# Output projection: two plain tiles and eight pairs by seven products, in place of four and seven

## The reference, cut to what matters

```python
    m = g_a * (y_a @ w_proj_a) + g_b * (y_b @ w_proj_b)
    return x + gate * (m @ w_out), k, v
...
y_prompt = rmsnorm(x, final_g)
y_sample = rmsnorm(z, final_g)
```

## Time and profile before

| | us |
|---|---|
| median of 3 runs | 1726.87 (1726.21 to 1728.54) |
| the profiled execution's own time | 1724.92 |
| its span | 1723.1 |
| TensorE busy in the span | 1690.2 (98%) |
| VectorE busy | 1245.8 (72%) |
| ScalarE busy | 861.1 (50%) |
| GpSimd busy | 655.3 (38%) |

### The profile page before, as it was taken

One profiled execution on the slowest core, in us unless ns is written; L12 is line 12 of the kernel. 1 busy time (PEld: TensorE's weight loads), 2 busy tenths in 40 slices (PEclk: granted clock), 3 DMA queues, 4 the chain that ended last, 5 costly groups with the idle time before them and its releaser, 6 DMA issues.

```text
span 1723.1 us, 27518 instructions
## 1 busy us (share of the span) xinstructions
PE 1690.2 (98%) x9835; PEld 1434.0 (83%) x9835; DVE 1245.8 (72%) x1785; ACT 861.1 (50%) x1497; POOL 655.3 (38%) x509
## 2 busy tenths in 40 slices
PE   5999999999999999999999999999999999999998
PEld 3787888888899988878888888888988888888886
DVE  3785788788656858888687855777777665678776
ACT  3553444455577644434544437777779222333443
POOL 0044675565200027865555653224223100005443
PEclk9999999999999999999999999999999999999999
DMA  9443534333598725434333369888766777673442
GB/s 326 125 148 128 134 125 142 95 92 110 177 320 258 208 92 134 158 124 110 99 125 102 104 167 222 229 224 192 169 145 174 246 235 229 189 263 129 152 159 86
DMA packets 271644, 286.31 MB, mean 166 GB/s; under 512 B 49960, under 2 KB 217748, under 8 KB 268309
## 3 DMA queue, kind: packets, MB, share of 16 engines
q1 hardware_dynamic: 270146, 276.31, 53.6%
q10 hardware_dynamic: 1363, 8.24, 2.1%
HBM read 203.18 MB, written 81.30 MB: 165 GB/s over the span
## 4 chain that ended last, share of the span: by engine, by line
PE 93%; DMA 2%; DVE 1%; issue 1%; ACT 1%; SPq 1%; POOL 1%; ACTq 0%; POOLq 0%; DVEq 0%
PE banks L1803 45%; PE banks L2361 6%; PE banks L2939 4%; PE banks L2941 4%; PE banks L2940 4%; PE banks L3000 3%; PE banks L3001 3%; PE banks L2999 3%; PE banks L2325 2%; PE banks L1933 2%; PE banks L1932 2%; PE banks L1931 2%; PE banks L2331 2%; PE banks L2301 1%; PE banks L2302 1%
## 5 line engine op out<-in xcount | busy, mean ns | idle before, releaser
L1803 PE MATMUL banks<-a_hi,w_hi 128*128 128x512 f32 x1176 | 460.2, 391 | 1.1 <-ACT out_stage L1121 0.4
L1803 PE MATMUL banks<-a_hi,w_lo 128*128 128x512 f32 x1176 | 457.9, 389 | 0.0
L1803 PE MATMUL banks<-a_lo,w_hi 128*128 128x512 f32 x1176 | 457.7, 389 | 0.0
L1494 DVE SCALAR_TENSOR_TENSOR banks<-glu_out,taps,banks 128x1009 f32<-128x1009 f32 (+1 forms) x240 | 342.2, 1426 | 5.3
L1803 PEld LDWEIGHTS banks<-a_hi,w_hi 128*128 128x128 f32 x1176 | 220.8, 188 | 50.2 <-issue 4.0
L1803 PEld LDWEIGHTS banks<-a_hi,w_lo 128*128 128x128 f32 x1176 | 220.7, 188 | 46.5
L1803 PEld LDWEIGHTS banks<-a_lo,w_hi 128*128 128x128 f32 x1176 | 220.8, 188 | 45.2
L1005 POOL TENSOR_TENSOR t_raw<-w_raw 128x512 f32<-128x512 f32 x39 | 53.7, 1377 | 396.5 <-DMA w_raw<-in_w_in 390.3
L1413 DVE SCALAR_TENSOR_TENSOR w_lo<-w_raw,w_hi 128x1024 fp32r<-128x1024 f32 x84 | 112.0, 1334 | 106.4 <-ACT w_hi L1095 105.1
L959 POOL TENSOR_TENSOR w_lo<-t_raw,w_hi 128x1024 fp32r<-128x1024 f32 x70 | 171.5, 2458 | 28.1 <-ACT w_hi L1095 25.8
L2473 ACT ACTIVATE probs<-scores,stat 128x640 f32<-128x640 f32 (+2 forms) x128 | 106.7, 833 | 50.6 <-DVE stat L2395 49.2
(11 more groups left out here) (276 smaller groups left out, 3660.2 us busy)
## 6 DMA issues: line engine op xcount, KB each, us to landing
w_raw<-in_w_in SPq DMA_DIRECT2D x34, 1024.0 KB, 5.6
cw_raw<-in_w_in SPq DMA_DIRECT2D x44, 512.0 KB, 5.1
proj<-out_stage SPq DMA_DIRECT2D x80, 256.0 KB, 2.2
gates_in<-proj SPq DMA_DIRECT2D x64, 256.0 KB, 3.1
q_split<-q_rows SPq DMA_DIRECT2D x8, 1152.0 KB, 6.0
w_ada<-in_w_ada SPq DMA_DIRECT2D x8, 1024.0 KB, 10.9
w_raw<-in_w_in SPq DMA_DIRECT2D x16, 512.0 KB, 4.8
q_rows<-out_stage_r SPq DMA_DIRECT2D x64, 128.0 KB, 2.4
```

Source lines behind the costliest of these rows:

```text
L1494: op = dve.scalar_tensor_tensor(dst, src, by, dst, ALU.mult, ALU.add)
L1803: op = pe.matmul(out, x[w][:, b, k], y, start=(start and k == j == 0), stop=(k == H - 1 and j == 2), skip_group_check=not start)
```

## The change

One pair more, two plain tiles less. Plain are now tiles 14 and 15; tiles 16 and 17 (the context) are the last pair. The first 256 columns of m's block 4 stay in SBUF (`mo_hi` and `mo_lo` are half as large), its last 256 are stored to memory by `store_m`, and `load_m_pair` for the first two pairs waits for the stores of all five blocks. The operands of the first pair lie elsewhere: A11, S1 and A12 need no plain tile to be done, S2 and S3 the first, S4 and A22 the second. The order of the preparing calls on ScalarE, VectorE and GpSimd is rewritten, and the loads of the weight blocks and of x are issued among the stores of block 4. Some waits of the first pair for units that are no more are left out.

```diff
 RING = [4, 5, 0, 1, 2, 3]
-OUT_BANKS = [6, 7, 4, 5, 0, 1, 2, 3]
-OUT_TILES = list(range(14, NTOK)) + list(range(14))
-PLAIN = 4
-OUT_UNITS = [(0, 0), (0, 1), (1, 0), (1, 1), (2, 0), (2, 1), (3, 1), (3, 0)]
+OUT_BANKS = [6, 7, 2, 3]
+OUT_TILES = [14, 15] + list(range(14)) + [16, 17]
+PLAIN = 2
+OUT_UNITS = [(0, 0), (0, 1), (1, 1), (1, 0)]
 NU, NE = len(OUT_UNITS), (NTOK - PLAIN) // 2
...
 Z_AT = {(part, e): NU + 4 * e + i + 1 for e in range(NE) for i, part in enumerate(PARTS)}
-SLOT_TILE = {"A11": 0, "S1": 0, "S2": 1, "A12": 1, "S3": 2, "S4": 2, "A22": 3}
+SLOT_TILE = {"S2": 0, "S3": 0, "S4": 1, "A22": 1}
 SUMS = {"S1": ("A21", "A22"), "S2": ("S1", "A11"), "S3": ("A11", "A21"), "S4": ("A12", "S2")}
 T_SUMS = {"T1": ("B12", "B11"), "T3": ("B22", "B12"), "T2": ("B22", "T1"), "T4": ("B21", "T2")}
-T_HIGHS, T_LOWS = ["T1", "T3", "T2", "T4"], ["T1", "T3", "T2", "T4"]
+T_HIGHS, T_LOWS = ["T1", "T3", "T2", "T4"], ["T1", "T2", "T3", "T4"]
 POOL_SUMS = [("T2", 0), ("T4", 0)] + [(s, e) for e in range(NE) for s in ("S1", "S2", "S3", "S4")]
...
         (wo_hi, wo_lo, wo_raw)[h % 3][h // 3] = at(f"wo{h // 3}_{kind}", [P, KC, 512], where, dtype)
-    mo_hi, mo_lo = at("mo_hi", [P, 4, KC, P], X_AT + 16384, F32R), at("mo_lo", [P, 4, KC, P], ln_at, F32R)
+    mo_hi, mo_lo = at("mo_hi", [P, PLAIN, KC, P], X_AT + 16384, F32R), at("mo_lo", [P, PLAIN, KC, P], ln_at, F32R)
     w_half = {"B11": (0, 0), "B21": (0, 1), "B12": (1, 0), "B22": (1, 1)}
...
     t_hi, t_lo, s_raw = {}, {}, {}
-    for n, where in (("A11", X_AT + 16384), ("S1", ln_at), ("S2", X_AT + 20480), ("A12", ln_at + 4096), ("S3", X_AT + 24576),
-                     ("S4", ln_at + 8192), ("A22", X_AT + 28672)):
+    for n, where in (("A11", X_AT + 24576), ("S1", X_AT + 28672), ("S2", X_AT + 16384), ("A12", ln_at + 8192), ("S3", ln_at),
+                     ("S4", X_AT + 20480), ("A22", ln_at + 4096)):
         t_hi[n], t_lo[n] = at(f"mo_{n}_hi", [P, H, P], where, F32R), at(f"mo_{n}_lo", [P, H, P], where + 2048, F32R)
...
         col, w = MC[c]
+        first = P * PLAIN if c == 4 else 0
         sp.wait_ge(m_done, og + 1)
-        sp.dma_start(io.m[P * o:P * o + P, col:col + w], m_raw[:, og % MR, 0:w]).then_inc(m_out[og % MR], 16)
+        sp.dma_start(io.m[P * o:P * o + P, col + first:col + w], m_raw[:, og % MR, first:w]).then_inc(m_out[og % MR], 16)
 
...
             for r in range(MR):
-                sp.wait_ge(m_out[r], m_base[r] + 16 * 8 // MR * 4)
-        sp.dma_start(m_pair[e % 2][:], io.m[:, 2 * P * e:2 * P * e + 2 * P].rearrange("(k p) t -> p k t", p=P)).then_inc(rows_in[e % 2], 16)
+                sp.wait_ge(m_out[r], m_base[r] + 16 * 8 // MR * 5)
+        col = P * OUT_TILES[PLAIN + 2 * e]
+        sp.dma_start(m_pair[e % 2][:], io.m[:, col:col + 2 * P].rearrange("(k p) t -> p k t", p=P)).then_inc(rows_in[e % 2], 16)
 
...
                 load_x(sp, 0)
-            if c < 4:
-                store_m(sp, og)
-        sp.wait_ge(mm, 76)
-        sp.wait_ge(wo_hid, 4)
-        load_block(sp, "B11")
-        load_block(sp, "B12")
-        sp.wait_ge(g_done, 76)
-        load_x(sp, 1)
-        sp.wait_ge(g_done, 78)
-        load_x(sp, 2)
-        sp.wait_ge(mm, 80)
-        load_block(sp, "B22")
-        load_block(sp, "B21")
+            if og == 38:
+                sp.wait_ge(mm, 76)
+                sp.wait_ge(wo_hid, 4)
+                load_block(sp, "B11")
+                load_block(sp, "B12")
+                sp.wait_ge(g_done, 76)
+                load_x(sp, 1)
+            if og == 39:
+                sp.wait_ge(g_done, 78)
+                load_x(sp, 2)
+                sp.wait_ge(mm, 80)
+                load_block(sp, "B22")
+                load_block(sp, "B21")
+            store_m(sp, og)
         sp.wait_ge(g_done, 80)
...
         load_x(sp, 4)
+        sp.wait_ge(mm2, 3)
+        load_m_pair(sp, 1)
         for p in range(NTOK - 1):
-            if p == PLAIN - 1:
-                sp.wait_ge(mm2, 7)
-                load_m_pair(sp, 1)
             n = {-1: 2}.get(p - PLAIN, (p - PLAIN) // 2 + 3)
...
             pe.wait_ge(copied, copies(e - 1, 2))
-        if name == "P5" and e == 0:
-            pe.wait_ge(z_done, 4)
         if name in ("P6", "P2"):
...
         name = next(p for p, a, _ in BLOCK_PRODUCTS if a == n)
-        eng.wait_ge(mm2, OM_AT[name, e - 1] if e else 2 * SLOT_TILE[n] + 2)
+        if e:
+            eng.wait_ge(mm2, OM_AT[name, e - 1])
+        elif n in SLOT_TILE:
+            eng.wait_ge(mm2, 2 * SLOT_TILE[n] + 2)
 
...
         act.wait_ge(mm2, OM_AT["P1", e])
-        act.wait_ge(z_done, Z_AT["C11", e - 1] if e else 3)
+        if e:
+            act.wait_ge(z_done, Z_AT["C11", e - 1])
         act.activation(c11_at, sums_at[e % 2], ACT.Copy).then_inc(copied, 1)
...
         act.wait_ge(mm2, OM_AT["P6", e])
-        act.wait_ge(z_done, Z_AT["C12", e - 1] if e else 5)
+        if e:
+            act.wait_ge(z_done, Z_AT["C12", e - 1])
         act.activation(c12_at, sums_at[e % 2], ACT.Copy).then_inc(copied, 1)
...
                 act.wait_ge(m_done, 32 + o + 1)
-                act.activation(mo_hi[:, :, o], m_raw[:, o % MR].rearrange("p (t n) -> p t n", n=P), ACT.Copy).then_inc(m_hid, 1)
+                act.activation(mo_hi[:, :, o], m_raw[:, o % MR, 0:P * PLAIN].rearrange("p (t n) -> p t n", n=P), ACT.Copy).then_inc(m_hid, 1)
             for lt, a, b in turns(c):
...
         block_high(act, "T1")
+        block_high(act, "T3")
         square_unit(act, 0)
-        block_high(act, "T3")
+        token_high(act, "A11", 0)
         block_high(act, "T2")
         square_unit(act, 1)
-        token_high(act, "A11", 0)
         block_high(act, "T4")
...
         token_high(act, "S1", 0)
-        square_unit(act, 3)
         token_high(act, "S2", 0)
         token_high(act, "A12", 0)
-        square_unit(act, 4)
-        square_unit(act, 5)
         token_high(act, "S3", 0)
+        square_unit(act, 3)
         token_high(act, "S4", 0)
-        square_unit(act, 6)
-        square_unit(act, 7)
         token_high(act, "A22", 0)
...
         dve.wait_ge(m_hid, o + 1)
-        m = m_raw[:, o % MR].rearrange("p (t n) -> p t n", n=P)
+        m = m_raw[:, o % MR, 0:P * PLAIN].rearrange("p (t n) -> p t n", n=P)
         dve.tensor_tensor(mo_lo[:, :, o], m, mo_hi[:, :, o].bitcast(F32), ALU.subtract).then_inc(m_lod, 1)
...
                 dve.wait_ge(g_in[og % 3], g_base[og % 3] + 32 * (og // 3 + 1))
-                if MR <= og < 32 + MR:
+                if og >= MR:
                     dve.wait_ge(m_out[og % MR], m_base[og % MR] + 16 * (og // MR))
-                elif og >= 32 + MR:
+                if og >= 32 + MR:
                     dve.wait_ge(m_lod, og - 31 - MR)
...
         block_sum(dve, "T1", summed)
+        block_sum(dve, "T3", summed)
         unit(0)
-        block_sum(dve, "T3", summed)
+        token_low(dve, "A11", 0)
+        block_low(dve, "T1")
         unit(1)
-        block_low(dve, "T1")
+        block_low(dve, "T2")
+        unit(2)
+        token_low(dve, "S1", 0)
+        token_low(dve, "A12", 0)
         block_low(dve, "T3")
-        unit(2)
-        final(0)
         unit(3)
-        block_low(dve, "T2")
-        block_low(dve, "T4")
-        unit(4)
-        final(1)
-        token_low(dve, "A11", 0)
-        token_low(dve, "S1", 0)
-        unit(5)
-        token_low(dve, "A12", 0)
-        final(2)
-        unit(6)
         token_low(dve, "S2", 0)
...
         token_low(dve, "S4", 0)
-        unit(7)
+        block_low(dve, "T4")
         token_low(dve, "A22", 0)
+        final(0)
         for e in range(NE):
...
         block_sum(pool, "T2", pool_sum)
-        rms_of(0)
         pool.wait_ge(pool_sum, POOL_SUM_AT["T2", 0])
...
         token_sum(pool, "S1", 0)
+        token_sum(pool, "S2", 0)
+        token_sum(pool, "S3", 0)
+        rms_of(0)
+        token_sum(pool, "S4", 0)
         rms_of(1)
-        token_sum(pool, "S2", 0)
-        rms_of(2)
-        token_sum(pool, "S3", 0)
-        token_sum(pool, "S4", 0)
-        rms_of(3)
         for e in range(NE):
```

## The result

| | before | after |
|---|---|---|
| median, same chip | 1727.56 (1726.21 to 1729.83, 6 runs) | 1736.55 (1731.56 to 1737.47, 6 runs) |
| the profiled execution's own time | 1724.92 | 1735.75 |
| its span | 1723.1 | 1733.9 |

The change makes the kernel slower, by less than 1% but clear of the noise: the ratio is 1.0045 with a 95% interval of 1.0034 to 1.0056, +7.8 us (+5.9 to +9.7; the medians stand 9.0 apart). A second measurement gave 1.0052 (1.0040 to 1.0064). The forecast was 1733.1, with a range to 1737.0.

The account below looks back on a forecast made before the run. TensorE's matmuls were taken as the bound. Saving 2.84 us against stalls of 8.3 or 9.4 gave +5.5 or +6.6; +6.2 was taken, from a median of 1726.87 to 1733.1, range 1727.5 to 1737.0.

Parts of the forecast that it names:

- the case of the falling clock: Rival: TensorE's clock falls in the stalls, a product at 1.2 GHz takes up to 2.74 us more; +8 to +11, chance 0.14.
- The saving: On TensorE, two plain tiles (22.0 us) go and a pair (19.16 us) comes: 2.84 us less.
- Nothing is given back later: From P1 of the second pair the old period holds; VectorE catches up by the third pair, no later product waits.
- Transfers: Loads before the first pair: B22 lands at 1542.8, m's last store at 1546, the first m_pair at 1553.1.
- A11's low behind the T4 sum: On VectorE, A11's low is shut out by GpSimd's T4 sum until 1554.4 and done at 1555.1.
- P5 and the order of the port: First pair's P5 waits for S1's low: 2.3 us late, or 4.6 if GpSimd gets the shared port in between.
- turns by arrival: VectorE and GpSimd alternate at the shared port: P5 4.6, P6 4.1, P4 0.8 us late; stalls 9.4, time 1733.5.
- P6 and the copy: P6 waits for the copy of P1's sum, behind square 3 and two highs on ScalarE: another 4.2 us late.
- P7: P7 waits for the copy of P6's sum, behind the second pair's S1 high on ScalarE: 1.8 us more, or in time.
- the row's order: At the shared port, waiting GpSimd stays out over successive VectorE instructions: stalls 2.3, 4.2 and 1.8 us, time 1732.3.
- cover suffices: Rival: m_pair lands by 1549.7, A11's low isn't held up, P5 in time; stalls 1.2, total -1.6 us; chance 0.12.
- half of it: Rival: one of the two delays is milder, stalls of 3 to 6 us, 0 to +3.4, about 1728.5; chance 0.12.

Follow-up runs that it names:

- experiment 7: Changed kernel with the first m_pair load waiting only for the stores of blocks 0 to 3, not block 4's: 1736.64 us, ratio 1.0049.
- Experiment 1: Changed kernel with GpSimd's T4 sum cut to 128x256 of 128x2048: first plain to last matmul 182.85 us, against 185.90.
- Experiment 3: Changed kernel with P1's sum copied ahead of square 3 and S2's low ahead of T3's: first plain to last matmul 188.55 us, against 185.90.
- experiment 6: Changed kernel's two plain tiles and eight pairs with the preparation reordered, T4's sum on VectorE: 1726.49 us, ratio 0.9991 to the kernel before.
- experiment 2: Changed kernel with T4's sum moved from GpSimd to VectorE, behind unit 0: first plain to last matmul 183.91 us, against 185.90.
- 5: Changed kernel run once more, unchanged: 1736.8 us, ratio 1.0052 to the kernel before; first plain to last matmul 185.08 us.

## Why the prediction was right, and where its sizes were off

*The total.* By the ratio the change costs 7.8 us, inside the forecast's own +3.5 to +8.9. The median of 1736.55 stands 3.4 above the forecast median of 1733.1 and just above its own range (to 1735.8), where the prediction had put the case of the falling clock (1736.5). That it meets this figure so closely is luck, since that case asked for +8 to +11 from stalls and clock together. The trace shows what each gave: the stalls ahead of P5 and P6 that the forecast named, and on top of them a fall of the clock that it had left out of its sum.

*The saving* was right: P1 at +22.00, 12 matmuls less. *Nothing is given back later* was right: from the second pair on the old period holds, with no wait in the list.

*Transfers.* Counted from the first plain matmul, m_pair's load left at +8.99 where the last store's landing was put at 8.6, and A11's high ran at +14.26; forecast +15.7. B22 landed for T3's sum at +5.94, forecast +5.4. Right to within 1.5 us. The load itself took 5.2 us where 7.0 was taken; the prediction took 7.0 as the middle of three loads, while the load in the same place of the kernel before had taken 9.3. A landing 1.0 us earlier turned out not to matter (experiment 7).

*A11's low behind the T4 sum* was right (done at +18.18; forecast +17.7). Experiment 1 confirms it by taking the sum away, 7 by moving the high.

*P5 and the order of the port.* This is a term that was mis-sized. The forecast weighed an order taken from one row, z_var behind two lows (P5 2.3 late), against turns by arrival (4.6 late), and took 6.2 us in all between the two sums of 5.5 and 6.6. Measured is 4.68: turns. In the rows of after a waiting instruction gets the port when the running one ends, each time: A11's low behind the T4 sum, S1's sum ahead of T1's low. That an instruction holds the port to its end is what the Trainium skill ("SBUF — State Buffer", Who interferes with whom) states, and these rows agree with it; who gets the port next it doesn't say, the rows do. The row of before, in which z_var stayed out over two lows, remains unexplained: it was one case made into a habit. The forecast by turns misses no product's start by more than 0.3 us up to P6.

*P6 and the copy* were right: 4.21 against 4.2, in the place named. The turn order had 4.1. Experiment 3 adds what the prediction had only as 0.8 us ahead of P4: that VectorE's arrears stand close behind.

*P7* was in time, as the turn order had it, since its copy ran at once; the 1.8 us of the row's order did not come.

*The clock.* This term the forecast's sum had at nothing; it was kept as a rival of 0.14, at +8 to +11 in all. It did fall, in an idle time of 4.5 us, and the forecast should have carried it: the stalls that it had worked out itself (4.2 ahead of P6 in one order of the port, 4.6 and 4.1 in the other) are longer than the 3.5 after which the earlier trace rows show it down. In the trace it fell sooner than that, after 2.2 us. It cost less than the rival said. P5 lost 2.2 us while P6 waited for the copy anyway, P6 lost 1.64, and of that 0.8 stands in the place of the wait ahead of P4, which the forecast by turns had at 0.8. By turns the forecast was +6.6; + 1.64 - 0.8 + some 0.3 of small misses gives the 7.7.

*The rivals "cover suffices" and "half of it"* fell with the stalls measured: 8.9 us (4.68 and 4.21), where the one had 1.2 and the other 3 to 6. What m_pair ahead of the T4 sum would have given stays open. The cover does suffice in another order, as experiment 6 shows.

## What to carry to other kernels

When cover is halved, what hid behind it must be put in order by when its reader needs it, on every engine: the changed kernel's order costs 10.6 us of stalls and slow clock here, the same work sorted anew 1.0. A saving on the bounding engine is only as good as the busiest of its suppliers in that stretch: removing the wait that one sees (the copy) brought out the next (`sum_22`), and with it a fall of the clock that made the whole slower. And where two engines share a port, long work can be better placed on the one that does it faster, even if that one is the busier: so it was in experiment 2, and in 6 together with a new order.

## What the runs showed of the hardware that was not expected

- The shared port changes hands when the running instruction ends, and a long one on GpSimd (4.6 us) holds up one of 0.7 us on VectorE for its whole rest (3.25 and 4.31 us in two kernels); behind a token sum of 1.3 us it is 1.72.
- TensorE idle for 1.45, 1.46 and 1.50 us (experiments 2, 5 and 1) kept its full clock; idle for 3.28 (experiment 2), 3.43, 3.90, 4.48 and 4.64 us it came back at 0.50, with matmuls 0.43 us apart, for most of a product. The Trainium skill ("TensorE: Matmul & The Clock Gate", The HAM clock gate) has both levels and the fall in idleness, and the traces agree.
- How long TensorE had stood idle when the clock fell differs from case to case: 2.2 us in the changed kernel, 2.4 in experiment 2, 3.4 in 5, 3.8 in 1 and 4.4 in 7. So the 3.5 us of the earlier trace rows are one case and no limit below which a stall is safe. In the changed kernel, an idle time of 1.81 us ahead of P6 was over when the clock fell 1.0 us later, with TensorE at work. Whether the slow run of P5 just before had a part in that, no run here can tell.
- Up to the merge, two executions of the kernel before differ by 2.4 us, from there to the first plain matmul and behind it by 0.01 at most. In so long a kernel a stretch of the trace tells a change of 1 us that the total can't.
